# Gated DeltaNet layer on one core: base steps spread otherwise over the chunks, q's third tap behind the residual add and fourth behind r, four more products in front of k's turn

## The reference, cut to what matters

```python
h = rms_norm(x, norm_w) * (1 + scale) + shift           # adaLN from silu(c) @ ada_w
p = h @ w_in                                             # q, k, v, z, b, a
qkv = silu(causal_short_conv(qkv, conv_w))               # 4 taps per channel
q = l2_norm(q) * dk ** -0.5; k = l2_norm(k)
beta = sigmoid(b); g = -exp(a_log) * softplus(a + dt_bias)
A = strict_lower((k * beta) @ k.T * decay); tri = A + I  # per chunk
u, w = solve(tri, [v * beta, k * beta * exp(gc)])
# scan over chunks, S the state of a head:
v_new = u - w @ S
o = (q * exp(gc)) @ S + (q @ k.T * decay) @ v_new
S = S * exp(g_last) + (k * exp(g_last - gc)).T @ v_new
y = rms_norm(o, gdn_norm_w) * silu(z) @ w_out
out = rms_norm(x + gate * y, final_norm_w)
```

## Time and profile before

| | |
|---|---|
| median of 3 runs | 1222.18 us (1219.55 to 1223.29) |
| profiled execution | 1221.72 us, of which the span is 1219.9 us |
| PE busy | 1110.8 us, 91% of the span |
| DVE busy | 846.3 us, 69% |
| POOL busy | 588.8 us, 48% |
| ACT busy | 451.5 us, 37% |
| granted TensorE clock | 0.983 over the span, 1.00 in every stretch from 140 to 1150 us |
| from a c = 3 ks to the next unit's | 69.1 us for an odd unit, 70.2 us for an even unit |

### The profile page before, as it was taken

One profiled execution on the slowest core, in us unless ns is written; L12 is line 12 of the kernel. 1 busy time (PEld: TensorE's weight loads), 2 busy tenths in 40 slices (PEclk: granted clock), 3 DMA queues, 4 the chain that ended last, 5 costly groups with the idle time before them and its releaser, 6 DMA issues.

```text
span 1219.9 us, 19507 instructions
## 1 busy us (share of the span) xinstructions
PE 1110.8 (91%) x5628; PEld 908.8 (75%) x5628; DVE 846.3 (69%) x1888; ACT 451.5 (37%) x1038; POOL 588.8 (48%) x819
## 2 busy tenths in 40 slices
PE   3887899999999999999999999999999999999984
PEld 3775678777887778777787778787787777887763
DVE  4776685876758585776758586685858777585835
ACT  4641433343242433334343433324243333334333
POOL 2354544475344734465344744456343843456413
PEclk9898999999999999999999999999999999999988
DMA  9921312213122321123121321213212222213002
GB/s 311 317 61 55 79 40 62 57 52 80 40 61 56 80 55 48 51 69 81 39 62 39 82 69 35 62 46 89 56 49 52 63 69 54 62 39 96 21 35 121
DMA packets 150753, 88.30 MB, mean 72 GB/s; under 512 B 29446, under 2 KB 145320, under 8 KB 150696
## 3 DMA queue, kind: packets, MB, share of 16 engines
q1 hardware_dynamic: 150696, 87.73, 26.2%
HBM read 78.28 MB, written 9.44 MB: 72 GB/s over the span
## 4 chain that ended last, share of the span: by engine, by line
PE 63%; POOL 11%; DVE 11%; issue 10%; ACT 3%; DMA 1%; DVEq 1%; SPq 0%; ACTq 0%; POOLq 0%
PE bank L403 29%; PE bank L503 15%; POOL w_lo L1340 4%; DVE work L927 4%; POOL wo_lo L1347 4%; DVE y L960 3%; PE bank L547 2%; PE bank L557 2%; PE bank L463 2%; PE bank L560 2%; PE bank L585 1%; PE bank L535 1%; PE bank L539 1%; POOL w_raw L1354 1%; PE bank L488 1%
## 5 line engine op out<-in xcount | busy, mean ns | idle before, releaser
L1340 POOL TENSOR_TENSOR w_lo<-w_raw,w_hi 128x256 fp32r<-128x256 f32 x384 | 321.5, 867 | 284.8 <-ACT w_hi L682 284.8
L403 PE MATMUL bank<-h_hi,w_hi 128*128 128x512 f32 x760 | 311.6, 410 | 10.2 <-POOL w_lo L1340 10.2
L403 PE MATMUL bank<-h_hi,w_lo 128*128 128x512 f32 x760 | 309.3, 407 | 0.0
L403 PE MATMUL bank<-h_lo,w_hi 128*128 128x512 f32 x760 | 308.4, 406 | 0.0
L927 DVE SCALAR_TENSOR_TENSOR work<-pre,cw,work 128x512 f32<-128x512 f32 x192 | 174.1, 907 | 15.4 <-DVE work L924 5.4
L403 PEld LDWEIGHTS bank<-h_hi,w_hi 128*128 128x128 f32 x760 | 143.3, 189 | 41.3 <-POOL w_lo L1340 14.0
L403 PEld LDWEIGHTS bank<-h_hi,w_lo 128*128 128x128 f32 x760 | 143.2, 188 | 29.7 <-issue 0.2
L403 PEld LDWEIGHTS bank<-h_lo,w_hi 128*128 128x128 f32 x760 | 143.4, 189 | 28.2 <-issue 0.2
L1390 POOL TENSOR_TENSOR og_lo<-work,og_hi 128x256 fp32r<-128x256 f32 x64 | 47.1, 736 | 220.9 <-ACT og_hi L742 220.9
L708 ACT ACTIVATE work<-work 128x512 f32<-128x512 f32 x64 | 40.4, 631 | 285.3 <-DVE pre L937 137.7
L503 PE MATMUL bank<-wo_hi,og_hi 128*128 128x512 f32 x256 | 113.2, 442 | 16.3 <-DVE y L960 16.3
(11 more groups left out here) (176 smaller groups left out, 1869.8 us busy)
## 6 DMA issues: line engine op xcount, KB each, us to landing
w_raw<-in_gdn_w_in SPq DMA_DIRECT2D x96, 512.0 KB, 4.0
work<-in_ada_w SPq DMA_DIRECT2D x8, 1024.0 KB, 9.7
w_raw<-in_gdn_w_out SPq DMA_DIRECT2D x16, 512.0 KB, 3.3
y<-in_x SPq DMA_DIRECT2D x8, 512.0 KB, 9.1
work<-in_ada_w SPq DMA_DIRECT2D x8, 512.0 KB, 5.5
n_dram<-work SPq DMA_DIRECT2D x16, 256.0 KB, 3.4
out<-y SPq DMA_DIRECT2D x8, 512.0 KB, 2.6
t_dram<-work SPq DMA_DIRECT2D x16, 64.0 KB, 1.6
```

Of the source, the lines that this page charges most:

```text
L403: mm = nc.tensor.matmul(bank[m % 2][:, :], w[:, m % 2, k, :], h[:, k, half, :], start=(r == 0), stop=(r == MM - 1))
L1340: i = nc.gpsimd.tensor_tensor(w_lo[:, k % 2, j:j + 2, :], w_raw_k[:, k % 2, j:j + 2, :], w_hi[:, k % 2, j:j + 2, :].bitcast(F32), ALU.subt ...
```

## The change

Four things are edited.

1. **FILLS.** In the merge stage the second fill of level 1 goes from 10 to 14 products and that of level 2 from 6 to 2. The table for unit 0 (FILL_FIRST) keeps its merge stage.
2. **Base steps.** Before, steps 0 to 2 ran at the end of chunk 0, 3 to 6 in chunk 1 and 7 to 10 in chunk 2 and 11 to 14 in chunk 3, each behind r. After, BASE_STEPS puts 0 to 2 (with the memsets and the wait for `blk_in`) behind r of chunk 0, that is in front of its state update, 3 to 5 at the end of chunk 0, 6 to 8 in chunk 1, 9 and 10 in chunk 2 and 11 to 14 in chunk 3.
3. **q's taps.** Taps 2 and 3 stood in chunk 2 in front of the state update. Tap 2 now stands behind chunk 2's residual add, and tap 3 behind chunk 3's r, in front of the base steps.
4. **silu(3)** goes from the end of chunk 2 to the end of chunk 3, and its tanh on ScalarE from chunk 2 to chunk 3, behind og_high(2).

```diff
-        FILLS = (((12, 12), (10, 10), (6, 6)), 16, ((8, 8, 6), (8, 8, 6), (2, 2, 6), (2, 2, 6)), 8)
+        FILLS = (((12, 12), (10, 14), (6, 2)), 16, ((8, 8, 6), (8, 8, 6), (2, 2, 6), (2, 2, 6)), 8)
...
+        BASE_STEPS = ((0, 3), (6, 9), (9, 11), (11, 15), (3, 6))
...
-                    if not last and c == 2:
+                    if not last and c == 3:
                         tanh(u, 3, 1, cvq[:, other, :])
...
-                    else:
-                        invert_blocks(u + 1, 4 * c - 1, min(4 * c + 3, BLK - 1))
+                    if not last:
+                        if c == 3:
+                            conv(u, par, nxt, 1, range(3, 4))
+                        invert_blocks(u + 1, *BASE_STEPS[c])
                     if c > 0:
                         gate_o(u, c - 1)
-                    if not last and c == 2:
-                        conv(u, par, nxt, 1, range(2, 4))
...
                         if c == 0:
                             silu(u, 2, zt[:, 1, :], gate=True)
-                            invert_blocks(u + 1, 0, 3)
+                            invert_blocks(u + 1, *BASE_STEPS[NCH])
                         elif c == 1:
                             conv(u, par, nxt, 1, range(0, 2))
                         elif c == 2:
+                            conv(u, par, nxt, 1, range(2, 3))
+                        else:
                             silu(u, 3, cvq[:, other, :])
-                        else:
                             conv(u, par, nxt, 2)
```

## The result

The changed kernel takes 1201.56 us, the median of 4 runs (1200.92 to 1203.63), against 1221.10 before in the same comparison. The ratio is 0.9845, with a 95% interval from 0.9827 to 0.9862: 19.5 us faster, where 12.4 was forecast. A second set of runs of it gave 1201.38 and 0.9839. The profiled execution of the changed kernel has a span of 1201.8, against 1219.9.

The account below looks back on a forecast made before the run. TensorE was taken to bound the kernel, stalling mostly for VectorE. Odd units -14.9, even units +2.0 and unit 15 +0.5 gave -12.4 from 1221.7, or 1209.3, stated as 1209.5 us; range 1203 to 1216, wider range 1198 to 1222.

Parts of the forecast that it names:

- Taps out of the front of chunk 2's state update: Chunk 2, all 15 units: state update starts 2.0 us earlier, stalls at ks and output projection (1.57) go; gain 1.5.
- g: Gain per unit from moving the taps, up to the last output projection: reckoned 1.6 us, taken as 1.5, bounds 0.9 to 1.83.
- Four products in front of k's turn, odd units: Merge stage: 0.92 us more products cover the whole 0.63 stall at k's turn; gain 0.63 in each of 7 odd units.
- Four products, even units: Tile 3's first product: the wait for GpSimd grows from 0.73 to 1.65 us, so the gain is 0.
- Base steps in front of the state update: Chunk 0: free in odd units; in even ones late read and slow operations hold the state update, cost 1.75 us.
- e: Cost per even unit of base steps in front of chunk 0's state update: 1.75 us, bounds 0.1 to 2.65.
- large way to be wrong: Even units' state update not held, or the last output projection waiting over a microsecond for VectorE.
- The sum: Whole kernel: odd units -14.9, even units +2.0, unit 15 +0.5, together -12.4 us from 1221.7.
- unit 15: Last unit, merge level 2: no products left to cover VectorE's answer, of at most 0.92; cost +0.5 us, once.
- Rival A: Operations before the state update are not slowed: e is 0.1, sum -25.6, time 1196 us; chance 0.15.
- rival C: Slower: gate_o(3) comes later, g falls to 0.3, even units still pay 1.75; sum +5.6, 1227.3 us; chance 0.10.
- the lower bound: Least value of g, 0.9 us: slow operations stay slow, VectorE wins only its 0.2 of idle and the 0.56.

Follow-up runs that it names:

- e8: The kernel before with only the edits of q's taps and silu(3), fills and base steps left in place: 1191.97 us, ratio 0.9763.
- e1: The kernel before with the fills alone (14 and 2 products instead of 10 and 6): 1225.94 us against 1220.59, ratio 1.0042.
- e3: The changed kernel with the base steps put back nearly as before, fills, taps and silu(3) as changed: 1195.93 us, ratio 0.9790; run again 1197.16.
- e2: The changed kernel with the fills of before (10 and 6), base steps, taps and silu(3) as changed: 1202.69 us, ratio 0.9849.
- the second profile: The changed kernel, not edited further, run and profiled once more beside e3's kernel: 1201.38 us; the clock fell in 2 of 8 even units.
- e7: e3's kernel with the fills of 14 and 2 in odd units only, 10 and 6 in even ones: 1186.36 us, ratio 0.9722.

## Why the prediction was right where it was, and where it was not

**Taps out of the front of chunk 2's state update.** Right, and nearly right in size. The two stalls went. Their worth was put at 1.57; from chunk 2's last product (L560, L563) to chunk 3's, the gain is 2.05 (the distance of chunk 3's end from the unit's start fell by 3.17, that of chunk 2's by 1.12). The idle in brackets counts from a modelled end: a product is busy 0.40 but the next stands at 0.23, so each wait costs about 0.2 more than its bracket says, and there were two. VectorE's gate_o(3) then came 2.14 earlier in the unit, 0.98 beyond the 1.16 that TensorE had gained by the end of the merge stage, where 0.9 was forecast, and the last output projection waits 0.64 for it. This gives 2.79 - 1.16 = 1.63 for g, against 1.5 taken and 1.6 reckoned. e8 shows the taps alone at 1.7 and 2.3: in even units g was undersized, for there the last output projection waits only 0.3 for VectorE. The prediction read its last stall from an odd unit and took it for both.

**Four products in front of k's turn, odd units.** Right in mechanism, 0.63 forecast, 0.8 to 0.9 measured (e1, and e3 less e8), by the same 0.2. The unit of the rows gained another 0.3 at merge level 0: the first product of L472 stood 6.81 us from the last output projection and now stands 6.51 from it. That is scatter and no part of the change: this distance goes from 6.48 to 6.80 over the odd units of the kernel before, and from 6.48 to 6.87 after.

**Four products, even units.** This step failed. The prediction said that the wait for GpSimd grows from 0.73 to 1.65 and that the gain is 0. The wait became 2.03 to 2.29, for two reasons. TensorE got there 1.07 us earlier in the unit, not 0.92. And the end of GpSimd's split was taken as fixed, since its list is unchanged, but the split took 3.22, not 2.80: the earlier TensorE brought VectorE's silu(1) forward into it, and one GpSimd instruction was held. At full clock this already costs 0.1 to 0.5 a unit. And the step ended at the wait: what the clock does behind a wait of that length was not asked, though the trace of before had none over 1.44 there. e1 shows the price, 2 us in each even unit where the clock fell, and a kernel 5 us slower.

**Base steps in front of the state update.** The forecast of the mechanism was right and its size too: e2 shows the late read, the slow operations and a wait of 1.25, and e2 less e8 is 1.6 in even units, against e = 1.75. Four operations were slow, not five. In odd units the cost was 0, as forecast. The profiled execution of the whole change does not have it, since the clock drop came first; the second profile has it in most units. So the "large way to be wrong" that I named, no hold in even units, was seen in one execution, and the sum still held, because the clock's fall, which no term of it names, cost as much in its place. This part of the agreement is luck.

**The sum.** In the profiled executions the 14 units from 176.9 to 1152.1 now take 177.4 to 1133.5, so they gained 19.1, 7 x -2.73, against 7 x -1.88 forecast. Of the missing 0.85 in a pair, half lies in the odd unit (means 68.89 and 66.34, a gain of 2.55 where 2.13 was forecast: fills and taps each undersized by 0.2) and half in the even one (a gain of 0.18 where a loss of 0.25 was forecast: the taps gave 2.2 instead of 1.5, and fills and base steps, by way of the slow clock, took 2.0 instead of 1.75). What lies before 176.9 grew by 0.5, where 0.25 was put for unit 0, and what lies behind the last mark grew by 0.6, where 0.5 was put for unit 15. Together -18.1 by the spans, where the forecast was -12.4; the medians say -19.5. Rival A (1196) is nearer to the result than the forecast, 5.6 us off against 7.9. Its premise, that the operations in front of the state update are not slowed, is refuted by e2 and by the second profile; in the first profile they were fast, but only because the slow clock had put the next split behind them, at a price that A doesn't have. Two smaller slips: in rival C the total is 10.1 - 15 g by the prediction's own terms, not 11.3 - 15 g, so it is slower by over 0.3% once g is under 0.43; and the 0.2 and 0.56 of the lower bound add up to 0.76, not 0.9.

**Open.** What decides whether the clock falls behind such a wait. In units 2 to 14 of the twelve traces there are 36 waits for GpSimd of 2.00 to 2.35 us, and it fell behind 30 of them; behind the other 48, of at most 1.61, it never did. But within one execution it fell behind 2.12 and not behind another 2.12 (e3), and in the second profile of the changed kernel it fell behind 2.21 and held behind 2.25 and 2.27. In unit 0 of e1, e2 and e3 it fell at the same place with a wait of at most 0.18 there, 1.1 to 1.3 us behind ks, which had waited 1.75. No run separates the length of the wait from what went before it.

## What to carry to other kernels

When a change puts more work in front of a wait, ask not only whether the other engine's answer is hidden but what the wait grows to at the next hand-over, in every kind of unit; the fills were right for odd units and wrong for even ones, and one `if` on parity gave 9.6 us once the base steps stood back (e3 to e7). A change in several parts that gains 1.5% can hold a part that costs: the taps alone gain 2.4%. Sizes read from idle brackets are lower bounds on TensorE; add the difference between a product's busy time and its spacing. A cost that waits behind another, like the hold behind the slow clock, shows only when the first is taken away.

## What the runs showed of the hardware

A wait of TensorE of 2.00 to 2.35 us for GpSimd was followed in 30 of 36 cases by some 3.5 us at half the granted clock (products 0.42 apart instead of 0.23); behind waits of up to 1.61 us at the same place it was not seen in units 2 to 14.

VectorE and GpSimd held each other both ways. During a GpSimd split, small two-input operations of VectorE ran one to each GpSimd instruction, 0.66 instead of 0.18 (e2), and a copy of 128x3 took 0.69 instead of 0.16 (the changed kernel). And a two-input VectorE operation of 128x512 that started first held one GpSimd instruction at 1.16 to 1.23 instead of 0.72 to 0.75, which made a split of 2.80 one of 3.22.
